# One of four convolution chunks computed by GpSimd instead of VectorE, in a hybrid attention and convolution block

## What is computed

```python
a, g = jnp.split(u, 2, axis=-1)
z = a * jax.nn.sigmoid(g)
z = lax.conv_general_dilated(z, w_dw[:, None, :], window_strides=(1,), padding=[(CONV_KERNEL - 1, 0)],
    dimension_numbers=('NWC', 'WIO', 'NWC'), feature_group_count=CONV_WIDTH) + b_dw
z = layernorm(z, ln_g, ln_b)
return jax.nn.silu(z)
```

## Time and profile before

| | |
|---|---|
| median of 3 runs | 378.95 us |
| lowest, highest | 378.33, 379.4 us |
| span of the profiled execution | 376.7 us |
| TensorE matmul busy (PE) | 357.7 us, 95% |
| VectorE busy (DVE) | 245.9 us, 65% |
| ScalarE busy (ACT) | 174.7 us, 46% |
| GpSimd busy (POOL) | 9.6 us, 3% |
| HBM | 169 GB/s over the span |

### The profile page before, as it was taken

The page is one execution under the profiler, slowest core; times in us unless marked ns, Lnnn a source line. Parts: engine busy times, 40 slices in busy tenths (PEclk is TensorE's granted clock), DMA queues, the critical chain, the costliest instruction groups (busy, mean ns, idle before and its releaser), DMA issues.

```text
span 376.7 us, 5090 instructions
## 1 busy us (share of the span) xinstructions
PE 357.7 (95%) x2019; PEld 307.7 (82%) x2020; DVE 245.9 (65%) x298; ACT 174.7 (46%) x195; POOL 9.6 (3%) x18
## 2 busy tenths in 40 slices
PE   6999999999999869899999999999999999999993
PEld 3688888777788658688899989899898989989882
DVE  2883799698899966996574473653628356263734
ACT  3785455654484313443456243635515363342513
POOL 2000000000040000000000000000000000000000
PEclk9999999999999969999999999999999999999998
DMA  7999164343253532367363657182754829360002
GB/s 290 378 331 348 54 233 163 112 131 97 111 190 122 188 112 111 122 214 234 115 209 113 224 198 249 49 287 110 263 182 141 248 68 321 113 222 1 0 0 111
DMA packets 31865, 63.71 MB, mean 169 GB/s; under 512 B 1098, under 2 KB 1258, under 8 KB 31852
## 3 DMA queue, kind: packets, MB, share of 16 engines
q1 hardware_dynamic: 31548, 63.00, 49.8%
q10 hardware_dynamic: 304, 0.53, 0.4%
HBM read 62.48 MB, written 1.05 MB: 169 GB/s over the span
## 4 chain that ended last, share of the span: by engine, by line
PE 75%; DVE 19%; issue 2%; DMA 2%; ACT 1%; SPq 0%; POOLq 0%; POOL 0%; DVEq 0%
PE ps L769 15%; PE ps L773 15%; PE ps L770 15%; DVE conv L564 9%; PE ps L965 8%; PE ps L966 8%; PE ps L967 8%; DVE w_lo L527 5%; PE ps L756 3%; DMA raw<-in_w_in_dram 2%; PE ps L831 1%; DVE a_lo L539 1%; DVE smax L570 1%; DVE zn L641 1%; PE ps L834 0%
## 5 line engine op out<-in xcount | busy, mean ns | idle before, releaser
L769 PE MATMUL ps<-w_hi,a_lo 128*128 128x512 f32 x288 | 113.5, 394 | 2.8 <-DVE a_lo L539 2.2
L773 PE MATMUL ps<-w_lo,a_hi 128*128 128x512 f32 x288 | 112.3, 390 | 0.3 <-DVE w_lo L544 0.3
L770 PE MATMUL ps<-w_hi,a_hi 128*128 128x512 f32 x288 | 112.2, 390 | 0.0
L965 PE MATMUL ps<-b_lo,w_hi 128*128 128x256 f32 x256 | 72.6, 284 | 0.0
L966 PE MATMUL ps<-b_hi,w_hi 128*128 128x256 f32 x256 | 72.4, 283 | 0.0
L967 PE MATMUL ps<-b_hi,w_lo 128*128 128x256 f32 x256 | 72.4, 283 | 0.0
L722 DVE TENSOR_TENSOR w_lo<-raw,w_hi 128x2048 fp32r<-128x2048 f32 x28 | 63.5, 2291 | 11.1 <-ACT w_hi L501 11.1
L527 DVE TENSOR_TENSOR w_lo<-raw,w_hi 128x2048 fp32r<-128x2048 f32 x29 | 66.3, 2288 | 5.9 <-ACT w_hi L354 5.9
L354 ACT CAST w_hi<-raw 128x2048 fp32r<-128x2048 f32 (+1 forms) x30 | 56.3, 1884 | 25.5 <-PE ps L773 22.2
L769 PEld LDWEIGHTS ps<-w_hi,a_lo 128*128 128x128 f32 x288 | 54.2, 188 | 13.9 <-DVE w_hi L533 2.5
L773 PEld LDWEIGHTS ps<-w_lo,a_hi 128*128 128x128 f32 x288 | 54.0, 188 | 12.2 <-DVE w_lo L544 0.8
(11 more groups left out here) (113 smaller groups left out, 230.6 us busy)
## 6 DMA issues: line engine op xcount, KB each, us to landing
raw<-in_w_ff_dram SPq DMA_DIRECT2D x32, 1024.0 KB, 5.5
raw<-in_w_in_dram SPq DMA_DIRECT2D x17, 1024.0 KB, 5.3
raw<-in_w_out_dram SPq DMA_DIRECT2D x4, 1024.0 KB, 5.1
raw<-in_w_attn_up_dram SPq DMA_DIRECT2D x2, 1024.0 KB, 5.1
raw<-in_w_conv_pw_dram SPq DMA_DIRECT2D x2, 1024.0 KB, 5.7
res<-in_x_dram SPq DMA_DIRECT2D x2, 512.0 KB, 3.8
raw<-in_w_in_dram SPq DMA_DIRECT2D x2, 512.0 KB, 6.5
gfin_bc<-in_g_final_dram SPq DMA_DIRECT2D x1, 512.0 KB, 5.8
```

The source lines that it names most:

```text
L769: nc.tensor.matmul(dst, lo[:, tok], w_hi[:, slot, k], start=start, stop=False)
L770: nc.tensor.matmul(dst, hi[:, tok], w_hi[:, slot, k], start=False, stop=False)
L773: return nc.tensor.matmul(dst, hi[:, tok], w_lo[:, slot, k], start=False, stop=stop)
L965: nc.tensor.matmul(dst, w_hi[:, slot, k, cols], b_lo[:, kk], start=kk == 0, stop=False)
```

## The change

Chunk 3 (the last 128 channels) is computed by GpSimd. For tap 0 it uses one `tensor_scalar` with the bias; for each of the taps 1 to 30 a `tensor_scalar` (product into one of two buffers, which lie in `zn`) and a `tensor_tensor` (adding it to conv). The addition of a tap waits for the product of its own tap and for the sum before it. VectorE keeps chunks 0 to 2 (93 instructions), with a new table of shares; it has none left in step 16. TensorE waits at S_LN for both. GpSimd's difference of bias rows now stands behind its convolution.

```diff
-TAPS_AT = {4: 4, 5: 9, 6: 9, 7: 9, 8: 9, 9: 11, 10: 11, 11: 11, 12: 11, 13: 11, 14: 11, 15: 9, 16: 9}
-assert sum(TAPS_AT.values()) == TAPS * 4
+CD = 3
+TAPS_AT = {4: 3, 5: 8, 6: 8, 7: 8, 8: 8, 9: 9, 10: 9, 11: 9, 12: 9, 13: 9, 14: 8, 15: 5}
+assert sum(TAPS_AT.values()) == TAPS * CD
...
             inverse_root(0, ms[:, 0], 1)

+            pool.wait_ge(z_made, CC)
+            pool.wait_ge(vec_made, 2)
+            pool.wait_ge(const_made, 4)
+            c = CC - 1
+            nc.gpsimd.tensor_scalar(conv[:, c], z[:, c, 0:T], dw[:, c:c + 1], vec[:, V_BDW + c:V_BDW + c + 1],
+                                    ALU.mult, ALU.add).then_inc(conv_last, 1)
+            for tap in range(1, TAPS):
+                product = zn[:, tap % 2, 0:T]
+                nc.gpsimd.tensor_scalar(product, z[:, c, tap:tap + T], dw[:, tap * CC + c:tap * CC + c + 1], None,
+                                        ALU.mult).then_inc(conv_prod, 1)
+                pool.wait_ge(conv_prod, tap)
+                pool.wait_ge(conv_last, tap)
+                nc.gpsimd.tensor_tensor(conv[:, c], conv[:, c], product, ALU.add).then_inc(conv_last, 1)
+
+            pool.wait_ge(conv_last, TAPS)
             pool.wait_ge(bias_hi, 1)
...
                 for m in conv_share(step):
-                    tap, c = divmod(m, CC)
+                    tap, c = divmod(m, CD)
+                    w = tap * CC + c
...
-                        dve.wait_ge(conv_step, m - CC + 1)
-                        nc.vector.scalar_tensor_tensor(out=conv[:, c], in0=z[:, c, tap:tap + T], scalar=dw[:, m:m + 1],
+                        dve.wait_ge(conv_step, m - CD + 1)
+                        nc.vector.scalar_tensor_tensor(out=conv[:, c], in0=z[:, c, tap:tap + T], scalar=dw[:, w:w + 1],
...
                 if n == S_LN:

-                    pe.wait_ge(conv_step, TAPS * CC)
+                    pe.wait_ge(conv_step, TAPS * CD)
+                    pe.wait_ge(conv_last, TAPS)
```

More of the change, by code:

```diff
@@ L207, in build @@
         conv_step = sem("conv_step")
+        conv_prod = sem("conv_prod")
+        conv_last = sem("conv_last")
         conv_tr = sem("conv_tr")
```

## The result

The changed kernel takes 379.76 us (median of 20 runs, 379.18 to 381.2), the kernel before 378.00 (20 runs, 376.44 to 380.31). The ratio is 1.0048, 95% interval [1.0033, 1.0063]: slower by half a per cent. The forecast had the direction, but 8.8 us of it against 1.8 measured, and 387.8 us in a range from 381 that does not hold 379.8. Of that distance of 8.0 us, 1.0 lies in the starting point: the forecast stood on 378.95, the median of three runs. The profiled spans, by which the rest is reckoned, differ by 1.0 us (377.7 against 376.7).

What follows compares the result with a forecast made beforehand. TensorE was taken to bound the kernel except in one VectorE-bound stretch. 24.2 us paid less 4.3 and 2.9 gave +17.0, less 8.2 gave +8.8: 378.95 + 8.8 = 387.8 us, range 381 to 399.

Steps and rivals of the forecast that it cites:

- What bounds the kernel, and what the changed one gives back: TensorE bounds all but one stretch; ending its wait before the convolution's transposes, slow clock included, gives back 8.2 us.
- the slow clock: Behind TensorE's wait at conv's transposes: eight transposes at 1.97 against 0.89 us, plus 2.0 for matmuls, 3.1 us.
- the rival without exclusion: GpSimd overlaps VectorE's taps; score waits (1.6) and 8.2 us go: -9.8, 369.2 us; chance 0.11.
- That the engines exclude each other: VectorE instructions with two SBUF inputs and GpSimd's SBUF readers exclude each other throughout; each GpSimd instruction is charged to VectorE.
- What each addition costs VectorE: Each GpSimd addition in chunk 3 holds up VectorE 0.54 us, upper bound 0.70.
- What each multiplication costs VectorE: Each GpSimd multiplication in chunk 3 holds up VectorE 0.34 us; lower bound 0.21, upper 0.70.
- The nearest row in shape: A select over 128x256 at 0.40 us, 0.28 after taking off 0.12; the multiplication's price was set between them.
- How fast they come: In steps 4 to 11 one GpSimd instruction goes between two of VectorE's; chunk done by step 11, about 100 us.
- The mild form among the rivals: Two taps to one GpSimd instruction spread the 61 over later steps with slack: some 5 us less than the sum.
- The sum: At the last scores +24.2 - 4.3 (taps saved) - 2.9 (idle used) = +17.0 us; behind them -8.2; net +8.8.
- Waits in the changed kernel: First row maximum about 12.8 us later; TensorE stands some 10 us at the first probabilities' transposes, its clock cost taken as 0.
- the prediction's own sum for x us a pair: Net for x us per multiplication-addition pair: 30x - 2.5 - 7.2 - 8.2, zero at x = 0.60.

Runs made afterwards that it cites:

- The kernel without GpSimd: Changed kernel with GpSimd's share left out: chunk 3 of the convolution not computed, VectorE keeps its 93 instructions; 369.32 us, ratio to before 0.9769.
- the fills: Changed kernel with each of GpSimd's 61 instructions replaced by a 128x256 f32 fill, chunk 3 not computed; 369.09 us, ratio 0.9749.
- the kernel with additions alone: Changed kernel where GpSimd does one multiplication, then 30 additions of shifted z to conv, no products; 378.59 us.
- early taps: Kernel before with seven VectorE taps moved forward from steps 14 to 16 into steps 5 to 8; 374.95 us, ratio 0.9900.
- order: Kernel before with step 16's nine taps moved into step 15, so the last weight subtraction comes behind the last tap; 374.72 us, ratio 0.9927.

## Why the prediction was right and wrong

- **What bounds the kernel, and what the changed one gives back.** Right. Predicted -8.2 us behind the last scores, measured 5.26 + 2.86 = 8.1; no wait for conv_last, clock up at the transposes. Two slips did no harm: the slow clock was priced at 3.1 us from records of two different views (the next eight transposes take 1.03 us in the view that gives 1.97, which makes it 2.9), and VectorE's taps behind the last scores are 20 fewer and not 18, while TensorE was the bound there. Part of what comes back is the order and not GpSimd: with step 16's taps moved forward alone, the kernel before gained 2.9 us (377.66 to 374.72). The kernel without GpSimd gained 8.7 of the 9.8 us of the rival without exclusion.
- **That the engines exclude each other.** Right, by the single event of the earlier trace rows, and by the fills it is reading that does it.
- **What each addition costs VectorE.** 0.54 predicted, 0.49 measured.
- **What each multiplication costs VectorE.** This term was mis-sized: 0.34 predicted, 0.22 measured, 3.9 us over all of them; with the additions, 26.7 against 21.3 us, it is the largest part of the miss. The lower bound from the fills of the earlier trace rows was 0.21. The nearest row in shape misled: its fixed part lies outside the exclusion.
- **How fast they come.** This step failed: "one GpSimd instruction goes between two of VectorE's ... so the whole chunk is done by step 11, about 100 us". I had taken GpSimd's own time to be about what it holds VectorE up. A multiplication holds it up 0.22 us but lasts 0.92, so three taps pass for one pair, and the last addition starts at 113.2. One to one came only in the kernel with additions alone. The mild form among the rivals came near this pattern (two taps to one GpSimd instruction, here three to two), for another reason (GpSimd's waits for semaphores); I valued it at 5 us and gave it no chance of its own.
- **The sum.** Predicted 24.2 us paid ahead of the last scores. Paid in the trace: eight or nine taps a step cost 5.36 to 5.76 us, free ones 3.25 or 3.65; over steps 5 to 11 that is 38.7 - 24.0 = 14.7, with 0.25 in step 4 and 0.22 on one subtraction 15.2 us. Of the 9.0 us difference 5.4 are the price (30 x 0.71 = 21.3 against 26.7), 1.4 the two pairs that came after the last scores, and 2.2 what fell into gaps beyond the 2.5 that I gave them: 28 x 0.71 = 19.9, less 15.2, is 4.7. The 1.4 come from the slow cadence, and the 2.2 too, as far as can be argued: GpSimd was still at work in VectorE's pauses at 94 to 97 and 106 to 108 us. TensorE's slow clock on the scores, taken as 0, cost 1.2 (the idle before the third row maximum is 2.83 and was 1.68). 15.2 - 4.3 - 2.9 + 1.2 = +9.2 late, as measured, in place of +17.0.
- **Waits in the changed kernel.** Expected 10 us at the transposes of the first probabilities; it was 1.4 there, as the first row maximum came 3.9 us late and not 12.8, and 7.3 in four places. By then 12 pairs at 0.71 had passed and not 20 at 0.88.
- **The range.** With 0.71 us a pair the prediction's own sum for x us a pair (30x - 17.9) gives +3.4 us, 382.4, still inside. It left out the combination that came: a low price together with the slow cadence.
- **The direction.** Little merit: it is the small difference of 9.2 us late and 8.1 regained. Moving eight taps in the changed kernel turned it round (ratio 0.9969), and a constant in place of the weight made it vanish.

## What to carry to other kernels

Work of this kind moved from VectorE to GpSimd pays only where VectorE waits or reads PSUM at that time, and the pauses here were too short for it (the row maximum at 75.09, which reads PSUM, kept its 0.68 us beside an addition); elsewhere compare what the GpSimd instruction holds up (here 0.71 us a pair) with what it saves (0.40). How long an instruction lasts, how long it keeps the other engine out, and how many come in a stretch are three numbers; a forecast needs each. Before moving work to another engine, move it within its own: a shift of eleven taps between steps gave 6.6 us, most of the 8.7 that leaving out a quarter of the work could give.

## What I had not expected

- A multiplication by a per-partition scalar on GpSimd (128x256 f32) lasts 0.92 us alone, longer than an addition of two tensors (0.72), and yet excludes VectorE for 0.22 against 0.49. With a constant it lasts 0.85 and excludes 0.08 less.
- VectorE instructions with one SBUF tensor input are held up too: the first taps (tensor_scalar, 0.41 us) took 0.50 and 0.56 beside GpSimd's tap 0 and first multiplication, and the tiny scaling of row maxima (0.17 us) up to 0.65 in the kernel where both engines compute chunk 3.

```profile
44.23 0.50 DVE L579 TENSOR_SCALAR conv<-z,dw,vec 128x256 f32<-128x256 f32 x1
...
44.65 0.56 DVE L579 TENSOR_SCALAR conv<-z,dw,vec 128x256 f32<-128x256 f32 x1
```

```profile
78.31 0.65 DVE L593 TENSOR_SCALAR nbias<-smax 128x4 f32<-128x4 f32 x1
```

- TensorE's granted clock was at its lower level behind the wait of 5.13 us, stayed at the upper one after a wait of 2.31 us (early taps) or 2.87 (order) in the profiled executions, and fell in the changed kernel behind two waits of 1.4 us, 9.4 us apart (78.15 and 87.54): the transposes at 88.90 take 1.30 us against 0.83 a step later. Those two waits are both on ScalarE's probabilities. Which idle pattern decides was not tried by itself.
